# Modulation vectors of a fused two-model block: from eight small matrix products per feed-forward stage to accumulation on VectorE

## The reference, cut to what matters

```python
def swiglu_ffn(h, w_gate, w_up, w_down):
    return (jax.nn.silu(h @ w_gate) * (h @ w_up)) @ w_down
...
        mod_l = (jax.nn.silu(c) @ w_mod[layer] + b_mod[layer])[:, None, :]
        mod_c = jax.nn.silu(c_ctx) @ w_mod[layer] + b_mod[layer]
        sh1_l, sc1_l, g1_l, sh2_l, sc2_l, g2_l = jnp.split(mod_l, 6, axis=-1)
```

## Time and profile before

| what | before |
|---|---|
| time of the profiled execution | 2497.31 us |
| its span, first to last instruction | 2495.5 us |
| median of the three runs | 2499.73 us |
| PE busy | 2314.0 us (93%) |
| DVE busy | 1281.4 us (51%) |
| ACT busy | 689.8 us (28%) |
| mean granted TensorE clock | 0.972 of full |

### The profile page before, as it was taken

The page is one execution under the profiler, slowest core; times in us unless marked ns, Lnnn a source line. Parts: engine busy times, 40 slices in busy tenths (PEclk is TensorE's granted clock), DMA queues, the critical chain, the costliest instruction groups (busy, mean ns, idle before and its releaser), DMA issues.

```text
span 2495.5 us, 37267 instructions
## 1 busy us (share of the span) xinstructions
PE 2314.0 (93%) x14806; PEld 1624.4 (65%) x14806; DVE 1281.4 (51%) x2038; ACT 689.8 (28%) x945; POOL 110.7 (4%) x203
## 2 busy tenths in 40 slices
PE   8999999989999989999969999999988789988988
PEld 7888798879888788888765444333375644333333
DVE  5556655555556655572464566555578532111112
ACT  4334543343334543352221110000046411100100
POOL 1000100000000000000000000000000000000000
PEclk9999999999999999999989999999999989999999
DMA  9774538756765367742367999999932479999997
GB/s 327 254 250 147 154 110 272 244 186 226 260 224 160 96 234 270 255 148 88 91 227 288 407 404 411 409 409 409 388 116 85 184 277 410 413 408 410 415 417 307
DMA packets 237088, 673.23 MB, mean 270 GB/s; under 512 B 25709, under 2 KB 165245, under 8 KB 183584
## 3 DMA queue, kind: packets, MB, share of 16 engines
q1 hardware_dynamic: 213584, 642.82, 69.0%
q0 software_dynamic: 8208, 13.46, 1.9%
q10 hardware_dynamic: 15168, 15.16, 1.9%
HBM read 674.57 MB, written 4.29 MB: 272 GB/s over the span
## 4 chain that ended last, share of the span: by engine, by line
PE 68%; DMA 19%; DVE 7%; DVEq 2%; ACT 2%; issue 1%; ACTq 1%; SPq 0%
DMA raw<-in_w 19%; PE ps L739 14%; PE ps L740 14%; PE ps L741 14%; PE ps L1197 10%; PE ps L1215 4%; PE ps L753 2%; PE ps L1268 2%; PE ps L780 2%; DVE w_lo L1969 1%; PE ps L1190 1%; PE ps L1168 1%; PE ps L1207 1%; PE ps L1409 1%; PE ps L1417 1%
## 5 line engine op out<-in xcount | busy, mean ns | idle before, releaser
L1969 DVE TENSOR_TENSOR w_lo<-raw,w_hi 128x2048 fp32r<-128x2048 f32 x180 | 411.1, 2289 | 329.1 <-ACT w_hi L1459 328.6
L739 PE MATMUL ps<-t_hi,w_hi 128*128 128x256 f32 (+1 forms) x1568 | 455.9, 291 | 4.5 <-DVE w_lo L1969 4.4
L1459 ACT CAST w_hi<-raw 128x2048 fp32r<-128x2048 f32 x180 | 342.0, 1905 | 409.4 <-PE ps L741 394.3
L740 PE MATMUL ps<-t_lo,w_hi 128*128 128x256 f32 (+1 forms) x1568 | 453.9, 289 | 0.0
L741 PE MATMUL ps<-t_hi,w_lo 128*128 128x256 f32 (+1 forms) x1568 | 451.0, 288 | 0.0
L739 PE MATMUL ps<-w_hi,t_hi 128*128 128x256 f32 (+1 forms) x1088 | 350.4, 322 | 9.9 <-DVE t_lo L1969 7.7
L741 PE MATMUL ps<-w_hi,t_lo 128*128 128x256 f32 (+1 forms) x1088 | 349.6, 321 | 0.0
L740 PE MATMUL ps<-w_lo,t_hi 128*128 128x256 f32 (+1 forms) x1088 | 349.6, 321 | 0.0
L739 PEld LDWEIGHTS ps<-t_hi,w_hi 128*128 128x128 f32 x1568 | 296.4, 189 | 24.6 <-issue 13.4
L2683 DVE SCALAR_TENSOR_TENSOR work<-ps,work 128x512 f32<-128x512 f32 x64 | 48.0, 751 | 499.2 <-PE ps L1215 499.2
L741 PEld LDWEIGHTS ps<-t_hi,w_lo 128*128 128x128 f32 x1568 | 297.3, 190 | 4.6
(11 more groups left out here) (352 smaller groups left out, 2594.2 us busy)
## 6 DMA issues: line engine op xcount, KB each, us to landing
expert_ahead<-in_w SPq DMA_DIRECT2D x188, 1024.0 KB, 24.2
raw<-in_w SPq DMA_DIRECT2D x128, 1024.0 KB, 23.4
work<-in_w SPq DMA_DIRECT2D x60, 1024.0 KB, 25.6
work<-in_w_mod SPq DMA_DIRECT2D x32, 1536.0 KB, 6.6
raw<-in_ffn_w_gate SPq DMA_DIRECT2D x44, 1024.0 KB, 9.0
raw<-in_ffn_w_up SPq DMA_DIRECT2D x44, 1024.0 KB, 10.1
raw<-in_ffn_w_down SPq DMA_DIRECT2D x44, 1024.0 KB, 4.9
raw<-in_w_in SPq DMA_DIRECT2D x18, 1024.0 KB, 5.3
```

The lines of the kernel that those rows point to most:

```text
L739: pe.matmul(dst, a[0], b[0], start=start, stop=False)
L740: pe.matmul(dst, a[0], b[1], start=False, stop=False)
L1459: act.copy(slot(j)[0], src).then_inc(w_hi_ready, 1)
L1969: return dve.tensor_tensor(dst, src, hi.bitcast(F32), ALU.subtract)
```

## The change

A chunk is now a pair of row chunks by half of the columns: 256 rows by 1536 columns, the same 1.5 MB, still eight of them in a stage and still one `mod_raw`. DVE multiplies each row of a chunk by that row's condition value and adds it to a running sum, for each of the two conditions (s) and each of the two row chunks (k): four passes over 1536 columns beside each unit. After four chunks a half of the columns is finished, and PE sums it over the 128 partitions with a matrix `pick` of zeros and ones: two such products in a stage, behind units 6 and 10. `mod_free`, on which the next `mod_load` waits, is now raised by the last of DVE's four passes, which stand at three places of a unit's list. DVE's loop over units is written out.

```diff
-            def mod_load(f, kk):
+            def mod_load(f, i, v):
 
                 l, c0 = divmod(f * MOD_COLS, 6 * D)
-                sp.wait_ge(mod_free, KD * f + kk + 1)
-                sp.dma_start(mod_raw, A["w_mod_2"][l][bass.ds(kk * P, P), c0:c0 + MOD_COLS]).then_inc(mod_landed, 16)
+                sp.wait_ge(mod_free, KD * f + 4 * i + v + 1)
+                sp.dma_start(mod_raw.rearrange("p (k n) -> p k n", k=2),
+                             A["w_mod_2"][l][2 * P * v:2 * P * (v + 1), :].rearrange("(k p) n -> p k n", p=P)
+                             [:, :, bass.ds(i * MOD_HALF + c0, MOD_HALF)]).then_inc(mod_landed, 16)
...
-            def mod_product(f, u, kk, bank):
+            def mod_over_rows(f, half, u):
 
                 pe.wait_ge(act_ready, FF_UNITS * f + u)
-                pe.wait_ge(mod_landed, 16 * (KD * f + kk) + 16)
-                for a, n in ((0, BANK), (BANK, MOD_Q - BANK)):
+                pe.wait_ge(mod_acc_ready, 2 * f + half + 1)
+                for s in range(2):
                     for q in range(4):
-                        mm = pe.matmul(ps[32 * q:32 * q + 32, bank + a // BANK, 0:n], cond[:, kk, :],
-                                       mod_raw[:, q * MOD_Q + a:q * MOD_Q + a + n], start=True, stop=True)
-                mm.then_inc(mod_free, 1)
+                        mm = pe.matmul(ps[32 * q:32 * q + 32, 6, 0:MOD_PART], pick[:, s, :], mod_sum_part(half, s, q),
+                                       start=s == 0, stop=s == 1)
+                mm.then_inc(mod_summed, 1)
...
                 for u in range(2, 10):
-                    if u > 2:
-                        pe.wait_ge(mod_copied, KD * f + u - 2)
-                    gate_up(u, 3 * u - 1, u % 2, u - 2)
+                    if u == 7:
+                        pe.wait_ge(mod_copied, 2 * f + 1)
+                    gate_up(u, 3 * u - 1, u % 2)
+                    if u == 6:
+                        mod_over_rows(f, 0, u)
                     ffn_down(u - 1, p0 + 3 * u + 1, 3 * u + 1, 1 - u % 2)
-                pe.wait_ge(mod_copied, KD * f + KD)
                 gate_up(10, 29, 0)
                 ffn_down(9, p0 + 31, 31, 1)
+                mod_over_rows(f, 1, 10)
...
+                def mod_rows(kk, k, s):
+
+                    half, c = kk // 4, 2 * (kk % 4) + k
+                    n = 0
+                    for acc in mod_sums(half, s):
+                        width = acc.shape[1]
+                        src = mod_raw[:, k * MOD_HALF + n:k * MOD_HALF + n + width]
+                        if c == 0:
+                            e = dve.tensor_scalar(acc, src, cond[:, c, s:s + 1], None, ALU.mult)
+                        else:
+                            e = dve.scalar_tensor_tensor(acc, src, cond[:, c, s:s + 1], acc, ALU.mult, ALU.add)
+                        n += width
+                    return e
...
                 def unit(u, par, v):
 
                     split(p0 + 3 * u + 2, p0 + 3 * v + 2)
                     if 2 <= v <= 9:
-                        mod_add(u - 2, 6 - 2 * par)
+                        dve.wait_ge(mod_landed, 16 * (KD * f + u - 2) + 16)
+                        mod_rows(u - 2, 0, 0)
                     dve.wait_ge(silu_ready, FF_UNITS * f + u + 1)
...
+                    if v == 6:
+                        dve.wait_ge(bmod_landed, 128 * (f + 1))
+                        mod_add(0)
                     if v < 10:
                         split(p0 + 3 * u + 3, p0 + 3 * v + 3)
+                        if 2 <= v <= 9:
+                            mod_rows(u - 2, 0, 1)
                         split(p0 + 3 * u + 4, p0 + 3 * v + 4)
+                        if 2 <= v <= 9:
+                            dve.drain()
+                            mod_rows(u - 2, 1, 0)
+                            mod_rows(u - 2, 1, 1).then_inc(mod_free, 1)
+                            if v in (5, 9):
+                                dve.drain().then_inc(mod_acc_ready, 1)
```

More of the change, by code:

```diff
@@ L46 @@
 MOD_Q = MOD_COLS // 4
+MOD_HALF = MOD_COLS // 2
+MOD_PART = MOD_HALF // 4
 FF_UNITS = FF // PC
@@ L260, in build, with mod_sums, mod_sum_part @@
         mod_raw = w(R2, MOD_COLS)
-        cond = w(R2 + MOD_COLS, KD * 32).rearrange("p (k m) -> p k m", k=KD)
+        cond = w(R2 + MOD_COLS, KD * 2).rearrange("p (k m) -> p k m", k=KD)
+        pick = w(R2 + MOD_COLS + 64, 64).rearrange("p (s m) -> p s m", s=2)
+        def mod_sums(half, s):
+            if half == 0:
+                return (w(R0, 768), w(R0 + 3328, 768)) if s == 0 else (w(R0 + 1792, 1536),)
+            return once[:, s, 3072:3072 + 3 * MOD_PART], w(R0 + 1024 + s * MOD_PART, MOD_PART)
+        def mod_sum_part(half, s, q):
+            a = q * MOD_PART
+            for piece in mod_sums(half, s):
+                if a < piece.shape[1]:
+                    return piece[:, a:a + MOD_PART]
+                a -= piece.shape[1]
         sc_rows = w(R3, 2048).rearrange("p (s d) -> p s d", s=2)
@@ L381, in build @@
         cond_ready = sem("cond_ready")
+        mod_acc_ready = sem("mod_half_accumulated")
+        mod_summed = sem("mod_half_summed_over_rows")
         mod_copied = sem("mod_copied")
@@ L609, in ffn @@
                         unit(4 * i + 2 + v, 3 * v + 5)
-                        mod_load(f, 4 * i + v)
+                        mod_load(f, i, v)
                 unit(10, 29)
@@ L772, in _, with gate_up @@
             pe.wait_ge(ident_landed, 16)
-            def mod_product(f, u, kk, bank):
+            def mod_over_rows(f, half, u):
                 pe.wait_ge(act_ready, FF_UNITS * f + u)
-                pe.wait_ge(mod_landed, 16 * (KD * f + kk) + 16)
-                for a, n in ((0, BANK), (BANK, MOD_Q - BANK)):
+                pe.wait_ge(mod_acc_ready, 2 * f + half + 1)
+                for s in range(2):
                     for q in range(4):
-                        mm = pe.matmul(ps[32 * q:32 * q + 32, bank + a // BANK, 0:n], cond[:, kk, :],
-                                       mod_raw[:, q * MOD_Q + a:q * MOD_Q + a + n], start=True, stop=True)
-                mm.then_inc(mod_free, 1)
+                        mm = pe.matmul(ps[32 * q:32 * q + 32, 6, 0:MOD_PART], pick[:, s, :], mod_sum_part(half, s, q),
+                                       start=s == 0, stop=s == 1)
+                mm.then_inc(mod_summed, 1)
             def ffn(f, n):
                 p0 = G0[f"ffn{f}"]
-                def gate_up(u, j, par, mk=None):
+                def gate_up(u, j, par):
                     for half in range(2):
-                        if half and mk is not None:
-                            mod_product(f, u, mk, 6 - 2 * par)
                         p = p0 + (3 * u - 1 if j else 0) + half
@@ L818, in ffn @@
                 ffn_down(0, p0 + 4, 4, 0, start=True)
-                pe.wait_ge(cond_ready, 1)
                 for u in range(2, 10):
-                    if u > 2:
-                        pe.wait_ge(mod_copied, KD * f + u - 2)
-                    gate_up(u, 3 * u - 1, u % 2, u - 2)
+                    if u == 7:
[3 more added lines that the diff above has]
+                        mod_over_rows(f, 0, u)
                     ffn_down(u - 1, p0 + 3 * u + 1, 3 * u + 1, 1 - u % 2)
-                pe.wait_ge(mod_copied, KD * f + KD)
                 gate_up(10, 29, 0)
                 ffn_down(9, p0 + 31, 31, 1)
+                mod_over_rows(f, 1, 10)
                 pe.wait_ge(w_ready, p0 + 33)
@@ L1717, in _ @@
                 if l == 1:
-                    act.wait_ge(mod_stored, 64 * 2)
+                    act.wait_ge(mod_stored, 128 * 2)
                     load(xres[:, 2:4, :], A["ctx_2"][0].rearrange("(t p) d -> p t d", p=P), x_landed)
@@ L1765, in even @@
                 split(p + 11)
-                act.wait_ge(mod_stored, 64 * 4)
+                act.wait_ge(mod_stored, 128 * 4)
                 for s in (0, 1):
@@ L2007, in _ @@
             dve.memset(w(R3 + 3584, 512), 0.0)
+            dve.memset(pick[:, :, :], 0.0)
+            dve.drain()
+            for s in range(2):
+                dve.memset(pick[:, s, s:s + 1], 1.0)
             dve.memset(ones[:, :], 1.0).then_inc(ones_ready, 1)
@@ L2158, in ffn, with mod_add @@
                 p0 = G0[f"ffn{f}"]
[L2160 to L2164, removed]
+                def mod_rows(kk, k, s):
[10 more added lines that the diff above has]
+                    return e
+                def mod_add(half):
+                    dve.wait_ge(mod_summed, 2 * f + half + 1)
+                    sums = early[:, half * MOD_PART:(half + 1) * MOD_PART]
+                    dve.tensor_tensor(sums, sums, ps[:, 6, 0:MOD_PART], ALU.add).then_inc(mod_copied, 1)
                 def unit(u, par, v):
@@ L2178, in unit @@
                     rest(lo, g, hi).then_inc(act_ready, 1)
+                    if v == 6:
+                        dve.wait_ge(bmod_landed, 128 * (f + 1))
+                        mod_add(0)
                     if v < 10:
```

(30 more changed lines are left out.)

## The result

| what | before | after |
|---|---|---|
| median | 2499.39 us (4 runs, 2496.23 to 2500.72) | 2789.12 us (4 runs, 2783.28 to 2793.16) |
| profiled execution, its span | 2497.31, 2495.5 us | 2791.3, 2789.5 us |
| PE busy | 2314.0 us (93%) | 2341.0 us (84%) |
| mean granted TensorE clock | 0.972 | 0.925 |

The ratio is 1.1162, 95% interval 1.1149 to 1.1176: slower, by 290 us. The forecast was 2767 us in 2715 to 2840.

The account below looks back on a forecast made before the run. PE bound the kernel before; after the change, DVE's work and the late loads in series would. 2497.31 us plus 264.6 for four longer stages plus 5.4 for the fourth stage's context norm gave 2767 us, range 2715 to 2840.

Parts of the forecast that it names:

- The mechanism: DVE's last pass frees the chunk buffer; SP issues chunk and gate panel only then, so DVE and PE stand still.
- DVE's list: DVE's own work per unit (passes, three splits, activation, drains): 16.65 us in the mean of seven units.
- The passes by shape: DVE's passes priced at 1.033 ns a column and 0.222 us fixed: 7.20 or 7.48 us a unit.
- The trip: From DVE's unit end through chunk and panel issue, panel landing and ACT's cast to DVE's next split: 11.77 us.
- The mean period: Time from unit to unit, 11.77 + 16.65 = 28.42 us against 18.48 before, seven times per stage.
- the bounds: Upper side: panel landing at most 9.9 us from issue, 0.5 for chunk and semaphores; +1.4 us in 28 periods, +39.
- The clock: PE idles each period, so gate starts at 1.2 GHz, 8.8 instead of 5.6 us; costs only 2 us per stage end.
- Rival (d): Clock stays at 1.2 GHz through the units; PE becomes the bound, 5.3 us more per period, 2915 us; chance 0.03.
- (c): The four transfers share the engines, so the gate panel lands up to 6.1 us later: +171, 2938 us; chance 0.05.
- The gain on PE: PE loses eight products and gains two sums per stage: 9.7 us less work, 39 us in four stages.
- the stages' ends: PE's work after DVE's last period: the last down ends 12.7 us later, 18.6 in the fourth stage (5.4 us more).

Follow-up runs that it names:

- The order alone: Changed kernel with SP issuing the next unit's three panel loads ahead of the modulation chunk: 2591.09 us, ratio 1.0365.
- the pieces alone: Changed kernel with the chunk loaded in two pieces with own semaphores, both still ahead of the panels: 2738.33 us, ratio 1.0958.
- order and pieces: Changed kernel with panel loads ahead of the chunk and the chunk in two pieces with own semaphores: 2469.06 us, ratio 0.988.

## Why the prediction was right

**The mechanism held at each station.** SP's waits are for DVE, 28 times; ACT's cast waits for a landing where it waited for PE; DVE's first split waits for ACT; PE's share is 84%. The order alone gives back 198 us, the pieces alone 51, and both together 320, which turns the loss into a gain. So the passes are affordable. What the change could not pay was the place of the event that frees the chunk's buffer, in front of the panels.

**DVE's list** was forecast at 16.62 us in units 3 to 5 and 16.90 in 7 to 9, and measured 16.69 (83.74 to 100.43) and 16.94 (1315.60 to 1332.54). The passes by shape (count, busy us, mean ns, idle before) against forecasts of 1.41, 1.015, 1.81 and 0.62 us from the earlier trace rows:

```profile
L2194 DVE SCALAR_TENSOR_TENSOR expert_once<-work,expert_once 128x1152 f32<-128x1152 f32 x56 | 79.1, 1413 | 1.9 <-issue 0.4
L2194 DVE SCALAR_TENSOR_TENSOR work<-work 128x768 f32<-128x768 f32 x56 | 54.4, 1013 | 1.6
L2194 DVE SCALAR_TENSOR_TENSOR work<-work 128x1536 f32<-128x1536 f32 x28 | 50.7, 1811 | 0.0
L2194 DVE SCALAR_TENSOR_TENSOR work<-work 128x384 f32<-128x384 f32 x56 | 34.2, 611 | 0.0
```

**The trip** was forecast at 11.77 us and measured 11.96 and 13.04 in the rows above, 12.3 in the mean of 28. The gate panel behind a chunk took 8.6 to 10.7 us to land, 9.4 in the mean, where the forecast had the median of all gate panels, 9.0. The mean period is 28.92 us instead of 28.42. That is the term that was mis-sized, by 0.5 us in each of 28 units, within the bounds that the prediction had set for it. SP's waits of 22 us, where some 25 were forecast, fit the same picture: SP spends over 6 us on issuing the bunch before it comes to the next wait.

**The clock** fell and returned in each unit, as forecast, and the path went round it: in the changed kernel DVE and the loads bind while PE is slow. Rival (d) did not come. Nor did (c), which had the panel land up to 6.1 us later than 9.0: the longest took 10.7.

**The gain on PE** was forecast at 39 us if nothing else binds, and fell somewhat short. With order and pieces PE is busy without a gap for the 40 us shown above: the last output row of the fourth stage starts at 1064.2 us instead of 1098.8, 34.6 us earlier, and PE's busy time falls from 2314.0 to 2277.3 us.

**Where the other 24 us lie.** The profiled execution is 24 us over the forecast. The stages, from the first chunk to the first output row (the first from the start), grew by 69.8, 67.3, 68.7 and 76.4 us, 282 in all where 270 were forecast. The trip's 0.5 us in 28 units account for about these 12 us; the stages' ends were rough estimates. Between stages 4 us net were added: 5.5 us more ahead of the fourth, 1.2 less ahead of the second and third. Why is open. After the fourth stage 7 us more came, for which the forecast has no term. Of these, 5.7 lie between the context norm and the first expert's output. The faster kernel with order and pieces has 4.9 there too, so the late loads of the feed-forward stages are not their cause. In GpSimd's timeline of the changed kernel, the first gather for the experts leaves 10.0 us after its index copy:

```profile
1617.36 0.18 POOL L2936 COPY token_of_slot_col<-token_of_slot 64x1 uint32<-64x1 uint32 x1 [229.24 <-DVEq L2682]
1627.56 1.00 POOL L2938 DMA_INDIRECT work<-router_rows,token_of_slot_col  x1 [10.03 <-issue]
```

It was 7.4 us in the kernel before and 10.02 in the faster one. So 2.6 of the 5.7 us lie at this place; the rest was not placed, and the cause stays open.

## What to carry to other kernels

When work moves from one engine to another, look first at the event that frees its input buffer: at what point of the new engine's list it is raised, and which loads stand behind it in the queue that waits. Here the passes fitted. But SP's wait, which had ended in the middle of a unit, now ended with DVE's unit, and the panel that DVE needed next stood behind it. Put the loads that the path needs first ahead of the wait, and split the buffer so that it comes free in parts; each of the two alone left the kernel slower than before (by 3.7% and 9.6%), both together made it 1.2% faster.

## What had not been expected of the hardware

Issuing is not always short. When SP sent a chunk and three panels in a row, the first three took 0.37 to 0.44 us each to issue, and the third panel 4.52 us (72.80 us, above). In the next bunch of the changed kernel (from 101.26 us) the three panels took 0.59, 1.45 and 3.73 us. With a chunk in two pieces the third took 2.50 and 3.17 us (at 100.64 and 128.35 us). Here nothing waited on SP in that time. A list that needs SP soon after such a bunch would presumably wait; no run here shows it.
